# A hybrid encoder layer: attention whose scores are also computed keys by queries, with the maximum subtracted inside the product, values stationary, sums by GpSimd and a result kept transposed

## What is computed

```python
def attend_block(qb, k, v):
    s = jnp.einsum('bqhgd,bkhd->bhgqk', qb, k) * (HEAD_DIM ** -0.5)
    pr = jax.nn.softmax(s, axis=-1)
    return jnp.einsum('bhgqk,bkhd->bqhgd', pr, v)

def axial_gqa(pq, pk, pv, q_gain, k_gain, cos, sin):
    q = apply_axial_rope(rms_heads(_heads(pq.astype(F32)), q_gain), cos, sin)
    k = apply_axial_rope(rms_heads(_heads(pk.astype(F32)), k_gain), cos, sin)
    ...
# in the layer
    mix = jnp.concatenate([y_rwkv, y_attn], axis=-1) @ lp['w_out']
    x = layer_norm(DEEPNORM_ALPHA * x + mix, lp['ln1_g'], lp['ln1_b'])
```

## Time and profile before

| | |
|---|---|
| median of 3 runs | 3257.13 us (3246.21 to 3258.13) |
| profiled execution, its time | 3271.64 us |
| its span | 3269.9 us |
| share of the span: PE / PEld / DVE / ACT / POOL | 86% / 73% / 44% / 24% / 23% |
| mean granted TensorE clock | 0.905 |
| attend, first score to last product | 562 to 1065 us |
| mixout, first to last instruction | 1804 to 2040 us |

### The profile page before, as it was taken

The page is one execution under the profiler, slowest core; times in us unless marked ns, Lnnn a source line. Parts: engine busy times, 40 slices in busy tenths (PEclk is TensorE's granted clock), DMA queues, the critical chain, the costliest instruction groups (busy, mean ns, idle before and its releaser), DMA issues. The chain is left out here.

```text
span 3269.9 us, 61289 instructions
## 1 busy us (share of the span) xinstructions
PE 2796.8 (86%) x25620; PEld 2385.6 (73%) x25620; DVE 1426.5 (44%) x2337; ACT 794.1 (24%) x1439; POOL 763.8 (23%) x448
## 2 busy tenths in 40 slices
PE   2699887999999688888888298799999939999996
PEld 1588775555565588888887176699999939999995
DVE  5245355334444466665563366323223252232334
ACT  2112110223333233333332111221211122111121
POOL 3215033000000211111111355222222132232222
PEclk9999988558889789999998599799999969999998
DMA  4223121000000211111110443522122042222210
GB/s 148 67 66 95 55 80 66 14 14 14 13 6 8 73 43 52 53 51 52 52 42 19 143 139 104 157 61 73 51 64 71 7 149 71 64 64 64 64 38 39
DMA packets 206890, 204.66 MB, mean 63 GB/s; under 512 B 17286, under 2 KB 168966, under 8 KB 206698
## 3 DMA queue, kind: packets, MB, share of 16 engines
q1 hardware_dynamic: 206698, 201.82, 20.2%
HBM read 154.60 MB, written 47.18 MB: 62 GB/s over the span
## 5 line engine op out<-in xcount | busy, mean ns | idle before, releaser
L2184 POOL TENSOR_TENSOR ff_w_lo<-ff_w,ff_w_hi 128x1024 fp32r<-128x1024 f32 x132 | 313.7, 2400 | 755.2 <-ACT ff_w_hi L2211 565.4
L2344 PE MATMUL ff_gu<-ff_x_hi,ff_w_hi 128*128 128x384 f32 x1408 | 472.2, 335 | 2.8 <-DVE ff_x_lo L2264 2.8
L2344 PE MATMUL ff_gu<-ff_x_lo,ff_w_hi 128*128 128x384 f32 x1408 | 471.7, 335 | 0.0
L2344 PE MATMUL ff_gu<-ff_x_hi,ff_w_lo 128*128 128x384 f32 x1408 | 471.7, 335 | 0.0
L2275 DVE SCALAR_TENSOR_TENSOR ff_th<-ff_th,ff_gu 128x384 f32<-128x384 f32 x88 | 48.8, 555 | 581.2 <-ACT ff_th L2224 581.2
L2344 PEld LDWEIGHTS ff_gu<-ff_x_hi,ff_w_hi 128*128 128x128 f32 x1408 | 265.4, 188 | 4.4 <-DVE ff_x_lo L2264 3.6
L2344 PEld LDWEIGHTS ff_gu<-ff_x_hi,ff_w_lo 128*128 128x128 f32 x1408 | 265.4, 188 | 0.8
L2344 PEld LDWEIGHTS ff_gu<-ff_x_lo,ff_w_hi 128*128 128x128 f32 x1408 | 265.3, 188 | 0.0
L2289 DVE TENSOR_TENSOR ff_y<-ff_dn,ff_y 128x512 f32<-128x512 f32 x264 | 180.3, 690 | 136.5 <-PE ff_dn L2357 136.3
L1025 PE MATMUL at_S<-at_kT,at_qT 64*128 64x512 f32 x320 | 210.4, 778 | 0.8 <-DVE at_qT L933 0.8
L2357 PE MATMUL ff_dn<-ff_w_hi,ff_a_lo 128*128 128x512 f32 x528 | 205.8, 390 | 0.0
(11 more groups left out here) (244 smaller groups left out, 5102.4 us busy)
## 6 DMA issues: line engine op xcount, KB each, us to landing
ff_w<-in_w_ffn_in SPq DMA_DIRECT2D x88, 512.0 KB, 5.0
ff_w<-in_w_ffn_out SPq DMA_DIRECT2D x44, 512.0 KB, 3.8
sc_x<-scratch_chT SPq DMA_DIRECT2D x72, 256.0 KB, 3.3
pj_x<-in_x SPq DMA_DIRECT2D x13, 512.0 KB, 3.6
co_w<-in_w_in SPq DMA_DIRECT2D x13, 512.0 KB, 5.8
scratch_chT<-co_sh SPq DMA_DIRECT2D x8, 785.0 KB, 4.3
scratch_scan<-sc_out SPq DMA_DIRECT2D x24, 260.0 KB, 2.5
mo_sc<-scratch_scan SPq DMA_DIRECT2D x24, 260.0 KB, 2.9
```

Of the source, the lines that this page charges most:

```text
L2184: nc.gpsimd.tensor_tensor(w_lo[:, q, x, :], w[:, q, x, :], w_hi[:, q, x, :].bitcast(F32), ALU.subtract).then_inc(done, 1)
L2344: last = nc.tensor.matmul(gu[:, g, m, 0:GRP], ww[:, q, m, k * P:(k + 1) * P], xx[:, k, g * GRP:(g + 1) * GRP], start=(j == 0), stop=(j == ...
```

## The change

Scores are computed twice. **Queries by keys** (`score`, `at_S`), only to find the maximum: 128 queries by 264 (short) or 348 (long) key columns at a time, all in fp32r with the operands split in a high and a low half stacked on 128 rows (`Q1`, `K1`) and a second product of 64 rows (`Q2`, `K2`). **Keys by queries** (`score_t`, `at_ST`): 128 keys stationary, 512 queries moving, two products, of which the second has two more rows that carry ones beside the keys and minus the maximum (high and low part, `neg`) beside the queries, so the maximum is subtracted in the product. ACT's exponential then gives probabilities that already stand with keys on the partitions: no `turn`, no copies. `value` has the values stationary (64 columns) and 512 probability columns moving, in fp32, one head into each half of `at_O`. POOL adds the probability tiles in `acc`; `total` multiplies ones by `acc`, which puts the sum on all 64 partitions; DVE inverts 2 x 256 columns (`invert`) and multiplies (`finish`). The result is channels by tokens and stored so (`oT`).

A unit u is 2 heads by 512 queries: 4 of the short sequence, 8 of the long one. A unit has one step for the meta keys and one for each key tile (5 or 9). While unit u = s-1 is in its steps, the `score` products of unit s, 16 or 24 chunks, are spread over them (`share`), and `total` and `invert` of unit s-2 stand in steps 1 and 2. `place` below is ACT's, `most_of` and `invert` DVE's, `score`, `score_t` and `value` PE's, and the second `turn` is DVE's in `mixout`. There the attention's half of the channels is loaded as it is (`aT`), and only the other half is transposed.

```diff
+                def place(t, half):      
+                    act.wait_ge(q_turned, 2 * t + half + 1)
...
+                    nc.scalar.activation(Q1[:, t // 4, heads, cols], of[:, :].rearrange("p (h c) -> p h c", c=P), ACT.Copy)
+                    nc.scalar.activation(Q2[0:HEAD, t // 4, heads, cols], of[0:HEAD, :].rearrange("p (h c) -> p h c", c=P), ACT.Copy).then_inc(q_copied, 1)
...
+                def most_of(s, c):
+                    starts = unit_keys(s)[1]
+                    n = chunk0(s) + c
+                    dve.wait_ge(s_done, n + 1)
...
+                    nc.vector.tensor_reduce(top[:, s % 2, c // len(starts), c % len(starts):c % len(starts) + 1], S[:, n % 2, 0:unit_keys(s)[2]],
+                                            AX.X, ALU.max).then_inc(s_read, 1)
...
+                def invert(u, x):
+                    dve.wait_ge(total_done, u + 1)
...
+                    cols = slice(x * 256, (x + 1) * 256)
+                    nc.vector.reciprocal(inv[:, cols], R[:, cols]).then_inc(inv_done, 1)
...
+                for s in range(ATT_UNITS + 2):
+                    u = s - 1
+                    main = 0 <= u < ATT_UNITS
+                    for i in walk(s):
+                        if s >= 2 and i == (2 if main else 0):
+                            invert(s - 2, 0)
+                        for part in range(3):
+                            for c in share(s, i, part):
+                                most_of(s, c)
+                            if s >= 2 and i == (2 if main else 0) and part == 0:
+                                invert(s - 2, 1)
+                            if s >= 2 and i == (2 if main else 0) and part == 1:
+                                finish(s - 2)
...
+                def score(s, c):
...
+                    wait(pe, s_read, n - 1)
+                    nc.tensor.matmul(S[:, n % 2, 0:width], Q1[:, group, head, cols], K1[:, g, at:at + width], start=True, stop=False)
+                    nc.tensor.matmul(S[:, n % 2, 0:width], Q2[0:HEAD, group, head, cols], K2[0:HEAD, g, at:at + width], start=False, stop=True).then_inc(s_done, 1)
...
+                def score_t(u, i, h):
...
+                    wait(pe, exp_done, item(u, i, h) - 1)
+                    nc.tensor.matmul(ST[0:m, h, :], K1[:, g, keys], Q1[:, group, head, :], start=True, stop=False)
+                    nc.tensor.matmul(ST[0:m, h, :], K2[0:HEAD + 2, g, keys], Q2[0:HEAD + 2, group, head, :], start=False, stop=True).then_inc(st_done, 1)
...
+                def value(u, i):
+                    pe.wait_ge(exp_done, item(u, i, 1) + 1)
...
+                    for h in range(2):
...
+                        last = nc.tensor.matmul(O[h * HEAD:(h + 1) * HEAD, u % 2, :], v, p, start=(i == 0), stop=(i == n))
...
                 def load(t, q):
                     rows = bass.ds(t * P, P)
 
-                    hold(sp, tp_done, 2 * (t - 1), sp_passed)
+                    hold(sp, lo_done, 2 * (t - 1), sp_passed)
...
-                    sp.dma_start(mix[:, q, RW:D], d["mix"][rows, RW:D]).then_inc(in_loaded[q], 16)
+                    sp.dma_start(aT[:, q, :, :], d["oT"].rearrange("(k p) t -> p k t", p=P)[:, :, rows]).then_inc(in_loaded[q], 16)
...
                 def turn(t, q, i):
-                    for b in range(2):
-                        dve.wait_ge(hi_done, 2 * t + b + 1)
-                        nc.vector.tensor_tensor(m_lo[:, q, 4 * b:4 * b + 4, :], tp[:, b, :].rearrange("p (k c) -> p k c", k=4),
-                                                m_hi[:, q, 4 * b:4 * b + 4, :].bitcast(F32), ALU.subtract).then_inc(lo_done, 1)
+                    dve.wait_ge(hi_done, 2 * t + 1)
+                    wait(dve, product_done, t - 1)
+                    nc.vector.tensor_tensor(m_lo[:, q, 4:8, :], aT[:, q, :, :], m_hi[:, q, 4:8, :].bitcast(F32), ALU.subtract).then_inc(lo_done, 1)
+                    dve.wait_ge(hi_done, 2 * t + 2)
+                    nc.vector.tensor_tensor(m_lo[:, q, 0:4, :], tp[:, q, :].rearrange("p (k c) -> p k c", k=4),
+                                            m_hi[:, q, 0:4, :].bitcast(F32), ALU.subtract).then_inc(lo_done, 1)
```

More of the change, by code:

```diff
@@ L842, in attend, with key_cols @@
         vec = sem("at_vec")
[L843 to L855, removed]
+        turn_bank = lambda t, half: R if t < 4 and half else T
+        def key_cols(b):
+            return (slice(0, 512), slice(528, 1040), slice(1040, 1552), slice(META, META + N_META))[b]
         with nc.Block() as block:
@@ L873, in store, with load @@
[L873 to L884, removed]
+                def load(t):
+                    wait(sp, q_lo_done, t - 1)
+                    sp.dma_start(q_in[:, t % 2, :], d["qkv"][t * P:(t + 1) * P, 0:512]).then_inc(q_loaded[t % 2], 16)
@@ new lines, in _ @@
+                split(0)
+                split(1)
+                for e in range(8):
+                    act.wait_ge(k1_turned, e + 1)
+                    cols = key_cols(e // 2)
+                    of = (S, S, ST, ST)[e % 4]
+                    nc.scalar.activation(K1[:, e % 2, cols], of[:, e % 2, 0:cols.stop - cols.start], ACT.Copy).then_inc(k1_copied, 1)
+                for t in range(4):
+                    place(t, 0)
+                    place(t, 1)
+                    if t < 2:
+                        split(t + 2)
@@ new lines, in turn @@
+                def turn(t, half):
+                    pe.wait_ge(q_lo_done, t + 1)
+                    wait(pe, q_copied, 2 * t + half - (1 if t < 4 else 0))
+                    if t > 4:
+                        pe.wait_ge(row_copied, 2 * (t - 4))
+                    to = turn_bank(t, half)
+                    for x in range(4):
+                        last = nc.tensor.transpose(to[:, x * P:(x + 1) * P], q_split[:, t % 2, 4 * half + x, :, :].bitcast(F32).rearrange("p x c -> p (x c)"), ident[:, :])
+                    last.then_inc(q_turned, 1)
@@ new lines, in total @@
+                def total(u):
+                    pe.wait_ge(acc_done, 2 * tile0(u + 1))
+                    if u + 1 < ATT_UNITS:
+                        pe.wait_ge(row_copied, 2 * (u + 1) + 1)
+                    wait(pe, inv_done, 2 * u)
+                    for h in range(2):
+                        last = nc.tensor.matmul(R[h * HEAD:(h + 1) * HEAD, :], ones[:, :], acc[:, u % 2, h, :], start=True, stop=True)
+                    last.then_inc(total_done, 1)
+                pe.wait_ge(made, 3)
```

498 lines of the change are left out of this document (274 added, 224 removed).

## The result

The changed kernel takes 3328.2 us (median of four, 3312.9 to 3330.8) against 3257.6 for the kernel before: a ratio of 1.020, interval 1.014 to 1.026. It is slower, by 1.4 to 2.6%; the forecast was 3201. Its profiled execution took 3330.2 us, with a span of 3327.3.

What follows compares the result with a forecast made beforehand. PE, partly at 1.2 GHz, was taken to bound `attend`, a DVE and POOL loop `mixout`. Attention -109 and `mixout` +53 gave -56 us: profiled 3271.6 to 3216, less 14.5 for the median, 3201; own range 3160 to 3240, wider range 3135 to 3280.

Steps and rivals of the forecast that it cites:

- score chunks, two products each ... 8 x 24 x 0.32 = 73: Attention on PE: score chunks after the first unit's, 3 x 16 x 0.24 and 8 x 24 x 0.32, together 73 us.
- I take 0.12 for 264 and 0.16 for 348: PE's rates at 2.4 GHz: an fp32r product takes 0.12 us for 264 columns and 0.16 for 348.
- The clock: Attention: PE's clock starts low, 5 us, and drops now and then, 8 us.
- the clock in `attend` stays where it was: Rival, attention: mean clock stays 0.78, 308 us become 395, +74 us, result 3275; chance 0.10.
- The start: Start of attention: nothing overlaps, 44 us from 556.4 on, where before it took 5.7 to the first score.
- 20 for `invert`: Attention: a reciprocal of 256 columns takes 1.6 us and PE waits about 2 us in 10 units, 20 us.
- at the units' ends: Attention: PE waits for maximum, low part and row at each unit's end, 0.7 x 11 = 8 us.
- The end, from the last value: End of attention: sums, inversions, finish and store take 10 us from the last value to the scan's first DMA.
- The value pair: Attention on PE: the two fp32 products of `value` run at the same time, priced as one, 1.14 us.
- mixout: `mixout`: the held load puts its 6.5 us trip on DVE's loop; with 1.1 more, seven tiles pay, +53 us.
- the port term: `mixout`: `m_lo` of `aT` reads two SBUF operands beside POOL's `mo_x` and ends about 1.4 us later.
- Hidden after all: Rival, `mixout`: the load is hidden by other work or overlap, 3201 - 53 = 3148; chance 0.12.

Runs made afterwards that it cites:

- kernel 1: The changed kernel with the second product of each score chunk contracting 66 rows instead of 64, the two extra query rows zero: 3200.5 us, 0.982 of before.
- kernel 9: kernel 1 plus an added fp32 product of 66 rows and 8 columns behind each score chunk: 3262.2 and 3267.7 us.
- Kernel 2: The changed kernel with the `mo_aT` load given its own wait and semaphore, the four other loads released by the transposes as before: 3274.0 us.
- kernel 5: kernel 1 plus an added product of 64 rows and 8 columns behind each score chunk: 3334.7 us.
- kernel 4: The changed kernel with one product a score chunk (low keys left out of the maximum) and an own wait for the `mo_aT` load: 3132.5 us, 0.961.
- Kernels 3 and 7: 3: the changed kernel with one product a score chunk, 3186.6 us; 7: kernel 4 with `value(u, i - 1)` ahead of `row(s, 0)`, 3126.7 us.

## Why the prediction was wrong

- **The failed step** is "score chunks, two products each ... 8 x 24 x 0.32 = 73", and with it "I take 0.12 for 264 and 0.16 for 348". The columns were right (kernel 1 shows 0.16). What was missing is that the second product of a chunk has 64 rows beside neighbours of 66 and 128, and that its load and the next one then lie bare: 0.32 us a chunk more, 78 us.
- **I had the row and misread it.** The 0.32 instead of 0.23 ahead of `mo_G` I put down to fp32 coming after fp32r. `mo_G` has 64 rows, its neighbour 128. In kernel 9 an fp32 product of 66 rows starts 0.16 us behind 348 fp32r columns, on time. So the 0.09 is the price of the change of rows. I charged it to `value`, where a change of the other side (64 output columns after 128) costs as much (kernel 1: `value` starts 0.25 us behind the 348 columns, 854.47 to 854.72), and not to the 240 chunks. The Trainium skill, "TensorEngine Tiling (Array Packing)", section "Key Properties", says that a change of the tiling mode drains TensorE. If a product of 64 rows among taller ones is such a change, the trace agrees, with 0.09 us ahead of it and 0.11 on the product behind. I had not weighed it.
- **The clock** was priced at 13 us. By the estimate of experiment 1 it cost some 58 where kernel 1 lost 3. The rival "the clock in `attend` stays where it was" was named, with the argument against it that PE "runs gapless fp32r with 128 rows". The stream was not gapless. The two misses are one: with 66 rows instead of 64 both vanish. The Trainium skill, "TensorE: Matmul & The Clock Gate", section "A second HAM failure mode: psum-queue depth-cycling", tells of a kernel whose frequent very short idle times between matmuls made the clock swing between its levels. The trace agrees, 0.99 to 0.73 as pauses are added.
- **The other terms of attention** held, and together were too high. From the stage's first DMA to the scan's the forecast makes 410.5 us (548.53 to 959), kernel 1 takes 391.7. The start took 51.3 of them, where 51.9 was forecast (44 from 556.4 on). The clock lost 3 (13), PE's idle time in front of `at_S` chunks is 7.0 in all (20 for `invert`), and at the units' ends 2.6 (8). The end, from the last value, is 14.5 instead of 10, since PE waits 5.2 us for GpSimd's sums. That leaves some 313 for the products, forecast at 308. The reciprocal itself was well sized, 1.6 against the median of 1.75 below; but PE waits only 0.3 to 0.5 us for it in the last seven long units, not 2. In the changed kernel itself PE shows no such wait. Of the five DVE instructions shown for it ahead of the forecast, three are the unit before's (two inversions and the multiplication), the other two are maxima.

```profile
850.08 0.43 PE L1106 MATMUL at_S<-at_K,at_Q 128*128 128x348 f32 x1 [0.51 <-DVE at_top L1015]
```

The reciprocals of the changed kernel, by tile (duration in ns, lowest, median, highest):

```profile
L1031 DVE RECIPROCAL at_inv<-at_R x24: 1694/1748/1758, 647.2 to 1058.3; 128x256 f32<-128x256 f32 x24
```

- **The value pair**: right, 1.01 us from the first of four records to the next start, where 1.14 was priced together with what `value` adds in front.
- **mixout**: right in mechanism and size, +57.9 for +53: the wait 6.6 us in the mean instead of 6.5, 5 us more in tiles 3 and 4, the port term as worked out (`m_lo` ends 2.2 us after its start, in eight tiles instead of seven). Kernel 2 took 51 of it away and left about the port term. "Hidden after all" is out.
- The 3201 that the forecast gave is within 1 us of kernel 1. That is a coincidence: there attention and all ahead of it gained 132 and `mixout` still lost 58.

## What to carry to other kernels

When products are mixed, list the rows and output columns of each stationary operand in order: here a product of 64 rows among taller ones left two weight loads bare, 0.32 us each time, and two rows of zeros bought that back. Price short products from a row with the same neighbours, not by their columns. And ask of the pauses on PE what they do to the clock: in this stage 80 us of them cost 140 (kernel 5). A load released by the last reader of its slot is on the path if the loop's first instruction needs it; give each buffer its own wait.

## What the runs showed that I had not expected

- A product of 64 rows between taller ones costs the same with 8 columns as with 348, at 2.4 GHz: 0.09 us ahead of it, 0.19 to 0.20 until the next start, and 0.11 on that one. The change from fp32r to fp32 costs nothing ahead (0.16 us behind 348 columns in kernel 9).
- The clock's mean in the stage follows the distance between products in steps as small as 0.2 us: 0.99, 0.97, 0.92, 0.85, 0.82, 0.73 for steps of 3.10 to 4.35 us, with PE busy nearly throughout. Within one kernel it isn't even: the changed kernel holds 2.4 GHz from 888 to 1055, with the same steps that ran at half before. Why there and not earlier stays open; no run separated it.
- A small DVE instruction, `at_neg` on 8 columns (0.17 us mostly), took 1.12 to 1.15 us beside GpSimd's additions at four units of kernel 4. Kernels 3 and 7 show it too. It was seen, not tested.
